# Routing with router weights in four column groups, the expert order by VectorE's maximum, and expert weights on GpSimd

## The reference

```python
g_prob = softmax(ht @ w_rg + b_rg)          # 4 groups; ht: 256 x 1024, normalised
g_val, g_idx = top_k(g_prob, 1)             # one group a token
e_in = (ht @ w_re + b_re)[token, g_idx]     # the group's 4 experts
e_val, e_idx = top_k(softmax(e_in), 2)      # two experts a token
gate = g_val * e_val / sum(e_val)
...
hid = silu(ht @ w_gate[e]) * (ht @ w_up[e]) * combine[:, e]
out = sum over e of hid @ w_down[e]
...
x = x + sigmoid(h3 @ w_pg) * (p @ w_ple)
```

## Time and profile before

| | |
|---|---|
| three runs | 774.41, 777.22, 778.81 us; median 777.22 |
| the profiled execution | 775.51 us, its span 773.8 us |
| TensorE / VectorE / ScalarE / GpSimd busy | 763.5 / 557.0 / 470.2 / 29.8 us |
| granted TensorE clock | 1.0 |
| loads | 149.60 MB at a mean of 193 GB/s |
| from the first expert load to the output | 568.6 to 773.8 us |

### The profile page before, as it was taken

How to read it: one execution, slowest core, us unless ns; L and a number is a source line. 1 busy time by engine, 2 the same in 40 slices (tenths; PEclk the granted TensorE clock), 3 DMA queues, 4 the chain that set the end, 5 groups by cost and what they waited for, 6 DMA issues and landing times.

```text
span 773.8 us, 12132 instructions
## 1 busy us (share of the span) xinstructions
PE 763.5 (99%) x4830; PEld 647.3 (84%) x4830; DVE 557.0 (72%) x665; ACT 470.2 (61%) x583; POOL 29.8 (4%) x64
## 2 busy tenths in 40 slices
PE   8999999999999999999999999999999999999998
PEld 8989878888998978888888998888887787877887
DVE  6789796575779697567578777458589485848875
ACT  6875597544586668654478635534476473737655
POOL 5400000000000000300000000000000000000000
PEclk9999999999999999999999999999999999999999
DMA  8556343656447435455645345654059797969931
GB/s 282 173 201 222 108 157 126 201 175 214 124 135 234 163 110 167 160 195 169 228 127 179 132 161 166 212 171 159 1 190 343 249 366 248 364 242 356 351 118 54
DMA packets 70040, 149.60 MB, mean 193 GB/s; under 512 B 8458, under 2 KB 11104, under 8 KB 69984
## 3 DMA queue, kind: packets, MB, share of 16 engines
q1 hardware_dynamic: 69568, 148.78, 56.2%
q0 software_dynamic: 384, 0.04, 0.2%
q10 hardware_dynamic: 32, 0.01, 0.0%
HBM read 147.76 MB, written 1.05 MB: 192 GB/s over the span
## 4 chain that ended last, share of the span: by engine, by line
PE 88%; DVE 4%; ACT 3%; DMA 3%; issue 1%; SPq 1%; DVEq 0%; ACTq 0%
PE mm L639 18%; PE mm L641 17%; PE mm L640 17%; PE mm L655 3%; PE mm L656 3%; PE mm L657 3%; PE aux L750 3%; PE aux L1162 3%; PE aux L1164 3%; PE aux L1163 3%; DVE sb_w_lo L1788 2%; DMA sb_raw<-in_w_in 2%; PE aux L1146 1%; PE aux L639 1%; PE aux L641 1%; PE aux L640 1%
## 5 line engine op out<-in xcount | busy, mean ns | idle before, releaser
L1788 DVE TENSOR_TENSOR sb_w_lo<-sb_raw,sb_w_hi 128x2048 fp32r<-128x2048 f32 (+2 forms) x148 | 306.5, 2080 | 89.6 <-ACT sb_w_hi L1286 43.3
L1286 ACT ACTIVATE sb_w_hi<-sb_raw 128x2048 fp32r<-128x2048 f32 (+1 forms) x83 | 155.3, 1872 | 114.6 <-PE mm L641 83.1
L639 PE MATMUL mm<-sb_w_hi,sb_hT_hi 128*128 128x512 f32 (+1 forms) x456 | 175.7, 385 | 2.1 <-DVE sb_w_lo L1788 2.1
L641 PE MATMUL mm<-sb_w_hi,sb_hT_lo 128*128 128x512 f32 (+1 forms) x456 | 172.6, 379 | 0.0
L640 PE MATMUL mm<-sb_w_lo,sb_hT_hi 128*128 128x512 f32 (+1 forms) x456 | 172.6, 379 | 0.0
L1626 ACT ACTIVATE sb_w_hi<-sb_raw 128x2048 fp32r<-128x2048 f32 x44 | 84.2, 1917 | 42.9 <-DMA sb_raw<-in_w_up 26.3
L639 PEld LDWEIGHTS mm<-sb_w_hi,sb_hT_hi 128*128 128x128 f32 x456 | 85.8, 188 | 19.7 <-issue 3.0
L641 PEld LDWEIGHTS mm<-sb_w_hi,sb_hT_lo 128*128 128x128 f32 x456 | 85.8, 188 | 16.3
L640 PEld LDWEIGHTS mm<-sb_w_lo,sb_hT_hi 128*128 128x128 f32 x456 | 85.9, 188 | 15.0
L655 PE MATMUL mm<-sb_hT_hi,sb_w_hi 128*128 128x256 f32 x272 | 78.3, 288 | 0.0
L656 PE MATMUL mm<-sb_hT_lo,sb_w_hi 128*128 128x256 f32 x272 | 76.9, 283 | 0.0
(11 more groups left out here) (413 smaller groups left out, 1137.8 us busy)
## 6 DMA issues: line engine op xcount, KB each, us to landing
sb_raw<-in_w_in SPq DMA_DIRECT2D x120, 512.0 KB, 4.6
sb_raw<-in_w_down SPq DMA_DIRECT2D x32, 512.0 KB, 5.9
sb_raw<-in_w_gate SPq DMA_DIRECT2D x31, 512.0 KB, 5.3
sb_raw<-in_w_up SPq DMA_DIRECT2D x31, 512.0 KB, 6.7
sb_raw<-in_w_out SPq DMA_DIRECT2D x16, 512.0 KB, 4.2
sb_raw<-in_w_up_attn SPq DMA_DIRECT2D x8, 512.0 KB, 4.2
sb_raw<-in_w_up_hgrn SPq DMA_DIRECT2D x8, 512.0 KB, 4.2
sb_raw<-in_w_o SPq DMA_DIRECT2D x8, 512.0 KB, 4.1
```

The costliest lines, as they stand in the source:

```text
L639: pe.matmul(dst, a_hi, rhs[0], start=start, stop=False, skip_group_check=True)
L641: return pe.matmul(dst, a_lo, rhs[0], start=False, stop=stop, skip_group_check=True)
L1286: act.activation(w_hi[:, slot(t), 0:width], raw[:, slot(t), 0:width], ACT.Copy).then_inc(hi_split, 1)
L1788: return dve.tensor_tensor(out_, a, b, op)
```

## The change

1. The router's weights are widened to 32 columns (12 of them zero) and multiplied by x's gain once, so that `xT` is a plain copy. They are the stationary side now: four tiles of the width stand in four column groups of 32, x's 256 tokens move. This leaves partial sums of the 20 logits on 4x32 partitions. VectorE copies them out (`logits_T`) and a product with `fold` (four stacked unit matrices) adds and transposes them.
2. o1 is added to x in two token halves; the second transposes, squares and copies follow by halves. The w_ple products are put between them in quarters.
3. The group is found by a maximum, a comparison, a scan (for ties) and a mask in place of `places`.
4. The order comes from VectorE's `max` and `max_index` on the counts; GpSimd's four operations for it go.
5. ScalarE makes all of x's second high half, GpSimd both of its low halves (`late_low`).
6. The gather goes by pairs of columns (`gather_ready` four times), and the splits of expert 0's quarters are put between the gathered pairs. Eight dummy products before expert 0 go, six are put before the gather.
7. VectorE's `expert_weights` ends with the shares; GpSimd does the rest, 14 operations in six links. `slot_products` goes from within expert 0's last quarter to between expert 0 and 1.

TensorE:

```diff
-        pe.wait_ge(in_small, 16 * 5)
-    for tt in range(TT):
-        for k in range(4 * half, 4 * half + 4):
-            last = pe.matmul(logits_at[:, tt * W:tt * W + 20], xT[:, k, tt * P:(tt + 1) * P], wr[:, k, :],
-                             start=k == 0, stop=k == KT - 1, skip_group_check=True)
+        pe.wait_ge(S["wr_ready"], 1)
+    pe.wait_ge(S["xT_ready"], 2 * half + 2)
+    for j in range(4):
+        k = 4 * half + j
+        last = pe.matmul(logits_at[32 * j:32 * j + 32, 0:256], wr[:, k, :], xT[:, k, :],
+                         start=half == 0, stop=half == 1, skip_group_check=True)
     if half == 1:
         last.then_inc(S["router_ready"], 1)
+def add_parts():
+    pe.wait_ge(S["logits_T_ready"], 1)
+    for tt in range(TT):
+        last = pe.matmul(logits_at[:, W + 32 * tt:W + 32 * tt + 20], logits_T[:, tt * P:(tt + 1) * P], fold,
+                         start=True, stop=True, skip_group_check=True)
+    last.then_inc(S["logits_ready"], 1)
+def late_transposes():
+    ps = begin(job("R1"))
+    for tt in range(TT):
+        if tt == 0:
+            pe.wait_ge(S["x_part"], 1)
+        else:
+            pe.wait_ge(x_ready, 8)
+        for k in range(4):
+            last = pe.transpose(ps[:, k * 256 + tt * P:k * 256 + (tt + 1) * P], x[:, tt, (4 + k) * P:(5 + k) * P], ident[:])
+    end(job("R1"), last)
...
 router(0)
-x_transposes(job("R1"), 1, 8)
 pe.wait_ge(S["pT_lo_ready"], 1)
 pe.wait_ge(lo_split, TM + RING + 1)
-ple(0, 0)
+ple(0, 0, 0)
+late_transposes()
+ple(0, 0, 1)
+ple(0, 1, 0)
 router(1)
-ple(0, 1).then_inc(S["ple_done"], 1)
+ple(0, 1, 1).then_inc(S["ple_done"], 1)
+add_parts()
+ple(1, 0, 0)
+ple(1, 0, 1)
 ranks()
-ple(1, 0)
-ple(1, 1).then_inc(tile_done, 1)
+ple(1, 1, 0)
+ple(1, 1, 1).then_inc(tile_done, 1)
+keep_busy(6)
...
-    for i, (x_part, tt) in enumerate(((x_hi, 0), (x_hi, 1), (x_lo, 0), (x_lo, 1))):
-        if i == 3:
-            pe.wait_ge(S["x_lo_ready"], 3)
-        for k in range(4):
-            last = pe.matmul(mm[h][:, k * 256:(k + 1) * 256], x_part[:, tt, 4 * h + k, :], pick[:, tt, :],
-                             start=i == 0 and k % 2 == 0, stop=i == 3, skip_group_check=True)
-    last.then_inc(S["gather_ready"], 1)
+    for pair_ in range(2):
+        for i, (x_part, tt) in enumerate(((x_hi, 0), (x_hi, 1), (x_lo, 0), (x_lo, 1))):
+            for k in (2 * pair_, 2 * pair_ + 1):
+                last = pe.matmul(mm[h][:, k * 256:(k + 1) * 256], x_part[:, tt, 4 * h + k, :], pick[:, tt, :],
+                                 start=i == 0 and k % 2 == 0, stop=i == 3, skip_group_check=True)
+        last.then_inc(S["gather_ready"], 1)
...
-    if s == 0 and part == 0:
-        keep_busy(8)
...
-            if part == 1 and k == 3:
-                slot_products()
...
 for s in range(STEPS):
+    if s == 1:
+        slot_products()
     up(s, 0)
```

GpSimd:

```diff
-pool.wait_ge(S["at_ready"], 1)
-pool.tensor_tensor(at_group, is_at, group_id.unsqueeze(1).broadcast_to([P, 4, 4]), ALU.mult
-                   ).then_inc(S["order_chain"], 1)
-pool.wait_ge(S["order_chain"], 1)
-pool.tensor_tensor(pairs, at_group[:, :, 0:2], at_group[:, :, 2:4], ALU.add).then_inc(S["order_chain"], 1)
-pool.wait_ge(S["order_chain"], 2)
-pool.tensor_tensor(order, pairs[:, :, 0], pairs[:, :, 1], ALU.add).then_inc(S["order_chain"], 1)
-pool.wait_ge(S["order_chain"], 3)
-pool.tensor_copy(order_i, order[0:1, :]).then_inc(S["order_ready"], 1)
+def of_x(t, tt):
+    return t[:, tt, :, 64:128].rearrange("p k q -> p q k")
+def late_low(tt):
+    return pool.tensor_tensor(of_x(x_lo, tt), x[:, tt, W:2 * W].rearrange("p (q k) -> p q k", k=KT),
+                              of_x(x_hi, tt).bitcast(F32), ALU.subtract).then_inc(S["x_lo_ready"], 1)
+pool.wait_ge(S["x_hi_ready"], 2)
+late_low(0)
+pool.wait_ge(S["x_hi_ready"], 3)
+late_low(1)
+def weigh(ins):
+    weights_count[0] += 1
+    ins.then_inc(S["weights_chain"], 1)
+    pool.wait_ge(S["weights_chain"], weights_count[0])
+weights_count = [0]
+pool.wait_ge(S["shares_ready"], 1)
+taken = shifted.rearrange("p (s f) -> p s f", f=4)
+by_expert = taken.rearrange("p (t s) f -> p t s f", t=TT)[:, :, 1:5, :]
+for tt in range(TT):
+    ins = pool.tensor_tensor(full[:, tt], by_expert[:, tt], share[:, tt].unsqueeze(2).broadcast_to([P, 4, 4]), ALU.mult)
+weigh(ins)
+for tt in range(TT):
+    ins = pool.tensor_tensor(full[:, tt, 0:2], full[:, tt, 0:2], full[:, tt, 2:4], ALU.add)
+weigh(ins)
+for tt in range(TT):
+    ins = pool.tensor_tensor(four[:, tt], full[:, tt, 0], full[:, tt, 1], ALU.add)
+for tt in range(TT):
+    ins = pool.tensor_tensor(full2[:, tt], is_at, ghot[:, tt].unsqueeze(1).broadcast_to([P, 4, 4]), ALU.mult)
+weigh(ins)
+for tt in range(TT):
+    ins = pool.tensor_tensor(pairs[:, tt], full2[:, tt, :, 0:2], full2[:, tt, :, 2:4], ALU.add)
+weigh(ins)
+for tt in range(TT):
+    ins = pool.tensor_tensor(at_hot[:, tt], pairs[:, tt, :, 0], pairs[:, tt, :, 1], ALU.add)
+weigh(ins)
+for tt in range(TT):
+    ins = pool.tensor_tensor(weights[:, tt, 0:16].rearrange("p (j e) -> p j e", e=4),
+                             at_hot[:, tt].unsqueeze(2).broadcast_to([P, 4, 4]),
+                             four[:, tt].unsqueeze(1).broadcast_to([P, 4, 4]), ALU.mult)
+ins.then_inc(S["weights_ready"], 1)
 pool.wait_ge(hT_lo_ready, 7 * KT)
 pool.wait_ge(S["hid_ready"], 2)
```

ScalarE:

```diff
+def late_squares(tt):
+    return act.activation(E[0][:, tt * W:(tt + 1) * W], x[:, tt, W:2 * W], ACT.Square, accum_out=st[:, 2 + tt:3 + tt])
+act.wait_ge(S["x_part"], 1)
+late_squares(0)
+act.wait_ge(x_ready, 8)
+link(late_squares(1))
+root()
 router_in(1)
-squares(1, 8)
-root()
 x_high(1)
...
+def gathered_high(pair_):
+    act.wait_ge(S["gather_ready"], pair_ + 1)
+    for kk in (2 * pair_, 2 * pair_ + 1):
+        act.activation(hT_hi[:, kk, :], mm[kk // 4][:, kk % 4 * 256:(kk % 4 + 1) * 256], ACT.Copy,
+                       scale=ffn_gain[:, kk:kk + 1]).then_inc(hT_hi_ready, 1)
+gathered_high(0)
+act.wait_ge(tile_done, RING + slot_before(TM + 1) + 1)
+act.wait_ge(S["first_loaded0"], 32)
+high_quarter(TM + 1, 0)
+gathered_high(1)
+high_quarter(TM + 1, 1)
+act.wait_ge(S["first_loaded1"], 32)
+high_quarter(TM + 1, 2)
+high_quarter(TM + 1, 3)
+gathered_high(2)
+gathered_high(3)
```

VectorE (not shown: nine small operations near L2452 that prepare `wr`, `fold` and constants):

```diff
+def add_late(tt):
+    return tt_(x[:, tt, W:2 * W], x[:, tt, W:2 * W], mm[1][:, tt * W:(tt + 1) * W], ALU.add)
+dve.wait_ge(tile_done, LAST2["o1"] + RING + 1)
+add_late(0).then_inc(S["x_part"], 1)
+add_late(1).then_inc(x_ready, 1)
+dve.wait_ge(x_ready, 8)
+dve.sem_inc(mm_free[1], 1)
 router_in(1)
-link(dve.tensor_copy(of_x(x_hi, 0), x_half(0)))
-tt_(of_x(x_lo, 0), x_half(0), of_x(x_hi, 0).bitcast(F32), ALU.subtract).then_inc(S["x_lo_ready"], 1)
-dve.wait_ge(S["xT_ready"], 8)
 compute_r(4)
...
+dve.tensor_copy(logits_T, aux[AUX2.turn("R0")[0]][:, 0:256]).then_inc(S["logits_T_ready"], 1)
+dve.wait_ge(S["logits_ready"], 1)
...
-places(logits[:, :, 0:4], 1.0, full, full2, at_hot, ghot)
-dve.sem_inc(S["ghot_ready"], 1)
 link(dve.tensor_reduce(top, fives, AX, ALU.max))
+top_group = top.rearrange("p (t s) -> p t s", t=TT)[:, :, 0:1].broadcast_to([P, TT, 4])
+link(tt_(firsts.rearrange("p (t n) -> p t n", t=TT), logits[:, :, 0:4], top_group, ALU.is_equal))
+link(dve.tensor_tensor_scan(firsts_so_far, four_long, firsts, 0.0, ALU.mult, ALU.add))
+dve.scalar_tensor_tensor(out=ghot.rearrange("p t n -> p (t n)"), in0=firsts_so_far, scalar=1.0, in1=firsts,
+                         op0=ALU.is_equal, op1=ALU.mult).then_inc(S["ghot_ready"], 1)
...
-link(dve.scalar_tensor_tensor(out=unequal, in0=aux[1][:, 16:20], scalar=4.0, in1=group_id, op0=ALU.mult,
+link(dve.scalar_tensor_tensor(out=unequal[:, 0:4], in0=aux[1][:, 16:20], scalar=4.0, in1=group_id, op0=ALU.mult,
                               op1=ALU.subtract))
-of_g = unequal.unsqueeze(2).broadcast_to([P, 4, 4])
-of_h = unequal.unsqueeze(1).broadcast_to([P, 4, 4])
+link(dve.max(by_value, unequal))
+dve.max_index(order_i.bitcast(U32), by_value, unequal).then_inc(S["order_ready"], 1)
...
-tt_(is_at, by_size.unsqueeze(1).broadcast_to([P, 4, 4]), group_id.unsqueeze(2).broadcast_to([P, 4, 4]), ALU.is_equal
-    ).then_inc(S["at_ready"], 1)
...
-dve.wait_ge(S["x_hi_ready"], 2)
-tt_(of_x(x_lo, 1), x_half(1), of_x(x_hi, 1).bitcast(F32), ALU.subtract).then_inc(S["x_lo_ready"], 1)
...
-    link(tt_(full, by_expert, share.unsqueeze(3).broadcast_to([P, TT, 4, 4]), ALU.mult))
-    dve.wait_ge(S["at_ready"], 1)
-    for tt in range(TT):
-        dve.tensor_reduce(four[:, tt, :], full[:, tt].rearrange("p g e -> p e g"), AX, ALU.add)
-        ins = tt_(full2[:, tt], is_at, ghot[:, tt].unsqueeze(1).broadcast_to([P, 4, 4]), ALU.mult)
-    link(ins)
-    link(dve.tensor_reduce(at_hot, full2, AX, ALU.add))
-    for tt in range(TT):
-        tt_(weights[:, tt, 0:16].rearrange("p (j e) -> p j e", e=4),
-            at_hot[:, tt].unsqueeze(2).broadcast_to([P, 4, 4]), four[:, tt].unsqueeze(1).broadcast_to([P, 4, 4]),
-            ALU.mult)
-    dve.tensor_copy(weights[:, :, 16], r[:]).then_inc(S["weights_ready"], 1)
...
```

(54 more changed lines are left out.)

65 lines of the change are left out of this document (25 added, 40 removed).

## The result

The changed kernel takes 780.1 us (median of 6 runs, 779.1 to 780.8), the one before 776.6 us (6 runs, 774.4 to 778.8, the three above among them): ratio 1.0050, 95% interval 1.0032 to 1.0067. Its profiled execution took 779.6 us, with a span of 777.9 us; the one before had 773.8.

What follows compares the result with a forecast made beforehand. From slot products to first down product VectorE bounds the kernel, TensorE around it. Late weights add 3.2 us at the slot products' end, other terms nothing further: profiled 775.5 to 778.7, median 780.4, range 775.2 to 784.6.

Steps and rivals of the forecast that it cites:

- Router: New router halves on TensorE take 0.5 us; group known 0.6 us sooner if nothing blocks VectorE.
- Subtractions on GpSimd over the comparison: GpSimd's low halves of x block VectorE's comparison until 565.0; group at 565.6, a 0.7 us loss against before.
- Order: Maximum and index on VectorE at 0.2 us each; first expert load at about 568.0, 0.6 us earlier.
- Pick, gather, expert 0: Pick at 569.6, gather from 569.85, expert 0 from 573.75 with weights landed, done on TensorE at 584.65.
- Weights on GpSimd: GpSimd's 3.0 us chain stands behind VectorE's split; weights at 587.3, slot products end at 589.15, +3.2 us.
- No blocking: Rival (0.15): VectorE and GpSimd share nothing that counts; weights at 583.9, slot products end 585.6, -0.3 us, 776.9.
- only the weights wait: Rival (0.20): GpSimd's subtractions finish or yield before VectorE's comparison, pick 1.1 us sooner; +2.0 us, 779.2.
- long waits: Rival (0.12): subtractions of 2 us or GpSimd small operations at 0.5 us; group and weights later, +5 to +7, 783.5.
- the gain carries further: Rival (0.08): VectorE's run from slots to down product shortens and TensorE's saved work shows; -2.4 at most, 774.8.
- Slot products moved: Behind expert 0, TensorE waits 0.6 us for VectorE's copy; no further cost, as VectorE is the path there.
- the clock: Sign of being wrong: TensorE's granted clock, 1.00 before, falls in the new idle time, worse than the sum; no size.
- Sum: +3.2 us at the slot products' end, carried to the end; profiled execution 775.5 to 778.7, median 780.4.

Runs made afterwards that it cites:

- 7: The changed kernel with GpSimd's second subtraction (x_lo) held back until the group is known: 779.2 us, ratio 1.0049 to the kernel before.
- 8: The changed kernel with weights on VectorE, slot products inside expert 0's last quarter and GpSimd's second subtraction held back: 773.6 us, ratio 0.9971 to the kernel before.
- experiment 9: The changed kernel with weights on VectorE, slot products inside expert 0, maximum and index behind the slots' reduction: 776.1 us, ratio 1.0004 to the kernel before.
- 3: The changed kernel, weights still on GpSimd, with VectorE's split of the third expert tile behind the copy of the slots: 779.2 us, ratio 1.0046 to the kernel before.
- 1: The changed kernel with GpSimd's weights back on VectorE, slot products still behind expert 0: 775.8 us, ratio 0.9996 to the kernel before.
- 2: The changed kernel with weights back on VectorE and slot products back inside expert 0's last quarter: 774.7 us, ratio 0.9987 to the kernel before.

## Why the prediction was right, step by step

- **Router**: 0.57 us a half in the chain, estimate 0.5, bounds 0.47 and 0.94. 8 passes of 256 columns in 0.57 us are 0.071 us each, against 0.117 with two groups and 0.112 for a dummy pass of only 128 columns on the whole array. So passes in different column groups did overlap; how many at once these rows don't say. The Trainium skill (TensorEngine Tiling (Array Packing), Key Properties) states that different tiles can execute in parallel, and the 0.071 us agree. The prediction took the row of two groups as showing it already; by itself, 0.117 beside 0.112, that row doesn't.
- **Subtractions on GpSimd over the comparison**: forecast 562.4 to 565.0, measured 561.80 to 564.87. The end was right by two errors: the high halves came sooner, and each took 1.53 us, not 1.28. The group was known at 565.3 (565.6). Experiments 7 and 8 show the blocking by taking it away. The Trainium skill (SBUF — State Buffer, Who interferes with whom) states this exclusive lock, and the 1.04 and 2.34 us rows agree with it.
- **Order**: MAX8 and its index (0.17, 0.09 and 0.16) cost what small rows cost; first load 567.62 (568.0). **Pick, gather, expert 0**: gather 569.24 (569.85), expert 0 573.36 (573.75), done about 584.7 (584.65). I took the weights for landed and the gather for the bound; experiment 9 shows that the load is as late as the gather, so the order's lead was no side matter.
- **Weights on GpSimd**: the six links take 2.97 us alone (3.0), blocked by the split as forecast, done 586.5 (587.3), since two links were done before the split and not one, and the split ended 0.3 us sooner (584.6 for 584.9). TensorE waits 1.89 us (forecast 2.7); slot products end at 588.7 (589.15), +2.8 for +3.2. "No blocking" is refuted by 3 and 7, "only the weights wait" by the 1.04 us row; "long waits" by the subtractions, 1.53 us and not 2, and "the gain carries further" by the run to the down product, which got longer and not shorter.
- **Slot products moved, "costs nothing further"**: wrong; this is a term that the sum put at nothing. The prediction counted the 0.6 us wait (measured 0.71) as covered by VectorE. But behind the two waits twelve products took 0.43 us each and not 0.23, and TensorE, not VectorE, ended last: 15.05 us from the copy of the slots to the down product, where VectorE's run alone needs 13.1 to 13.5. That is 1.5 us beyond the +2.8. The prediction had named the clock as what could make it worse, but given it no price. The new place has a second cost, which the late weights hide in the changed kernel: with the weights in time (1 against 2) the copy of the slots comes 1.47 us later, because expert 0's last six products now stand ahead of the slot products, and VectorE's run starts that much later. Only the remaining 0.41 us of the 1.88 lie behind the copy.
- **Sum**: +3.2 us forecast, +3.9 by the ratio, +4.1 between the spans, +3.5 between the medians. That the median came out within 0.3 us of the forecast 780.4 is in part luck: the step was larger than forecast, and the median of the kernel before was 776.6 in the six runs and not 777.2. Two errors met inside the step too: the weights came early, which took 0.4 us off, and the clock put 1.5 us on at the down product.
